# Expert matrices read as neighbouring rows per partition, with a gather of every eighth feature, in a two-layer diffusion trunk

## The reference

```python
N_EXPERTS, N_GROUPS, EXPERTS_PER_GROUP, TOP_K, EXPERT_FF = 16, 4, 4, 2, 512

def moe_ffn(h, router_w, router_b, w1, w3, w2):      # w1, w3: (16, 1024, 512); w2: (16, 512, 1024)
    t = h.reshape(-1, shape[-1])                     # (256, 1024)
    gates = route(t, router_w, router_b)             # (256, 16), two entries not zero per token
    for e in range(N_EXPERTS):
        y = (jax.nn.silu(t @ w1[e]) * (t @ w3[e])) @ w2[e]
        out = out + gates[:, e:e + 1] * y

for i in range(DEPTH):                               # two layers
    x = x + g1 * mixer(...)                          # attention and short convolution, or Conformer convolution
    x = x + g2 * moe_ffn(modulate(rms_norm(x, norm2_g[i]), sh2, sc2), router_w, router_b, w1[i], w3[i], w2[i])
```

## Time and profile before

| | |
|---|---|
| median of 3 runs | 1104.04 us (1101.06 to 1104.61) |
| the profiled execution | 1102.05 us, its span 1100.3 us |
| TensorE matmul busy | 993.9 us, 90% of the span |
| TensorE weight load busy | 789.4 us, 72% |
| VectorE, ScalarE busy | 776.9 us (71%), 624.0 us (57%) |
| DMA | 300.83 MB, 273 GB/s on average |
| mean granted TensorE clock | 0.954 |

### The profile page before, as it was taken

How to read it: one execution, slowest core, us unless ns; L and a number is a source line. 1 busy time by engine, 2 the same in 40 slices (tenths; PEclk the granted TensorE clock), 3 DMA queues, 4 the chain that set the end, 5 groups by cost and what they waited for, 6 DMA issues and landing times.

```text
span 1100.3 us, 17266 instructions
## 1 busy us (share of the span) xinstructions
PE 993.9 (90%) x6128; PEld 789.4 (72%) x6128; DVE 776.9 (71%) x956; ACT 624.0 (57%) x762; POOL 86.9 (8%) x150
## 2 busy tenths in 40 slices
PE   3899989886999999999986998855999999999994
PEld 1588864755888888888864884835888888888873
DVE  1643278447998989989945534644998988978893
ACT  3523326225778778777733423323777778767672
POOL 4090000000000000000000632000000000000000
PEclk8899999997999999999998999876999999999998
DMA  9997864378999999999949965406998998997861
GB/s 336 327 276 227 266 216 137 133 276 280 361 345 310 353 348 317 358 317 351 349 152 361 264 201 178 153 0 212 336 351 318 352 347 312 353 356 236 283 248 40
DMA packets 143035, 300.83 MB, mean 273 GB/s; under 512 B 13461, under 2 KB 44325, under 8 KB 142962
## 3 DMA queue, kind: packets, MB, share of 16 engines
q1 hardware_dynamic: 135360, 286.53, 74.4%
q0 software_dynamic: 6080, 12.66, 4.1%
q10 hardware_dynamic: 1530, 0.78, 0.3%
HBM read 292.35 MB, written 2.92 MB: 268 GB/s over the span
## 4 chain that ended last, share of the span: by engine, by line
PE 81%; DVE 9%; DMA 3%; issue 3%; ACT 2%; SPq 0%; DVEq 0%; ACTq 0%
PE ps L1578 16%; PE ps L1580 16%; PE ps L1579 16%; PE ps L1829 3%; DMA raw<-in_w_mod 3%; PE ps L2051 3%; PE ps L1680 2%; PE ps L1682 2%; PE ps L1681 2%; PE ps L1590 2%; PE ps L1698 1%; PE ps L2073 1%; PE ps L2074 1%; PE ps L2075 1%; PE ps L1700 1%
## 5 line engine op out<-in xcount | busy, mean ns | idle before, releaser
L1318 DVE TENSOR_TENSOR wlo<-raw,whi 128x1024 fp32r<-128x1024 f32 x384 | 456.9, 1221 | 50.7 <-ACT whi L713 48.6
L713 ACT CAST whi<-raw 128x1024 fp32r<-128x1024 f32 x384 | 397.0, 1052 | 105.1 <-PE ps L1580 104.5
L1578 PE MATMUL ps<-whi,xghi 128*128 128x512 f32 x480 | 194.1, 404 | 13.7 <-DVE xglo L1324 13.7
L1580 PE MATMUL ps<-wlo,xghi 128*128 128x512 f32 x480 | 191.8, 400 | 0.0
L1579 PE MATMUL ps<-whi,xglo 128*128 128x512 f32 x480 | 191.8, 400 | 0.0
L1017 DVE TENSOR_TENSOR wlo<-raw,whi 128x1024 fp32r<-128x1024 f32 x56 | 73.8, 1359 | 62.2 <-ACT whi L708 62.2
L1578 PEld LDWEIGHTS ps<-whi,xghi 128*128 128x128 f32 x480 | 91.5, 191 | 35.5 <-issue 13.7
L1580 PEld LDWEIGHTS ps<-wlo,xghi 128*128 128x128 f32 x480 | 91.3, 190 | 22.1
L1579 PEld LDWEIGHTS ps<-whi,xglo 128*128 128x128 f32 x480 | 91.6, 191 | 21.2
L1578 PE MATMUL ps<-whi,hidThi 128*128 128x512 f32 x256 | 102.2, 399 | 1.4 <-issue 1.4
L1580 PE MATMUL ps<-wlo,hidThi 128*128 128x512 f32 x256 | 101.4, 396 | 0.0
(11 more groups left out here) (314 smaller groups left out, 1503.3 us busy)
## 6 DMA issues: line engine op xcount, KB each, us to landing
raw<-in_moe_w SPq DMA_DIRECT2D x384, 512.0 KB, 5.2
raw<-in_w_mod SPq DMA_DIRECT2D x96, 512.0 KB, 6.4
raw<-in_na_w_in SPq DMA_DIRECT2D x24, 512.0 KB, 9.0
raw<-in_cf_pw_w SPq DMA_DIRECT2D x24, 512.0 KB, 8.2
mods<-mod_scratch POOLq DMA_DIRECT2D x9, 512.0 KB, 5.0
raw<-in_ab_w_out SPq DMA_DIRECT2D x8, 512.0 KB, 4.8
urep<-uT SPq DMA_DIRECT2D x64, 35.5 KB, 3.3
urep<-uT POOLq DMA_DIRECT2D x64, 35.5 KB, 3.6
```

What stands on the lines that cost most here:

```text
L713: A.copy(whi[:, (MOE_W[tn.L] + j) % SPL, :], raw[:, (MOE_U[tn.L] + j) % RAW, :]).then_inc(tn.sem("w_rounded"), 1)
L1318: V.tensor_tensor(wlo[:, n % SPL, :], raw[:, (MOE_U[L] + j) % RAW, :], whi[:, n % SPL, :], ALU.subtract).then_inc(tn.sem("unit_done"), 1)
L1578: T.matmul(dst, lhi, rhi, start=first, stop=False)
L1580: return T.matmul(dst, lhi, rlo, start=False, stop=last)
```

## The change

The first and third matrices of the experts (w1, w3) are read so that partition p of chunk k holds feature 8p+k: a partition's share of a unit is two neighbouring rows, 4 KB in one run of device memory, and the runs of two partitions begin 16 KB apart. The gather follows: chunk k takes the features k, k+8, k+16 and so on, which puts 8p+k into partition p. The stationary operand of its matmuls is now a view of `htok` with a step of 8 floats.

```diff
                     else:
-                        src = src[0].rearrange("(k p) n -> p k n", p=P)[:, 2 * q:2 * q + 2, :]
+                        src = src[0].rearrange("(p k) n -> p k n", p=P)[:, 2 * q:2 * q + 2, :]
                         dst = raw[:, slot, :].rearrange("p (k n) -> p k n", k=2)
                     eng.dma_start(dst, src).then_inc(tn.loaded_sem(j), 16)
...
+                def every(t, k):
+
+                    return htok[:, t, :].rearrange("p (m k) -> p k m", k=KC)[:, k, :]
+
                 def gather(tile):
...
-                            ins = T.matmul(dst, htok[:, t, k * P:(k + 1) * P], sel, start=(t == 0), stop=(t == NT - 1))
+                            ins = T.matmul(dst, every(t, k), sel, start=(t == 0), stop=(t == NT - 1))
...
-                            ins = T.matmul(dst, htok[:, t, k * P:(k + 1) * P], pick[:, t, (GROUPS - 1 + e) * P:(GROUPS + e) * P],
+                            ins = T.matmul(dst, every(t, k), pick[:, t, (GROUPS - 1 + e) * P:(GROUPS + e) * P],
```

## The result

| | before | changed |
|---|---|---|
| median of 6 runs | 1104.1 us | 1145.88 us (1144.03 to 1150.33) |
| profiled execution, its span | 1102.05, 1100.3 us | 1144.03, 1142.3 us |
| mean granted TensorE clock | 0.954 | 0.956 |

The ratio is 1.0386, 95% interval 1.0362 to 1.0410: some 42 us slower. The forecast was no change (1103); the range ended at 1143. What happened is the first rival. The median lies 6 us above its estimate of 1140, the profiled execution 4 us; both are inside its 1134 to 1146.

A forecast was written before the change was run, and what follows sets the result against it. The prediction took TensorE to bound the kernel, with DMA hidden behind it. Its terms summed 0 + 0 + 0 + 0 on the profiled 1102.05 us, taken as 1103 us (no change, chance 0.52), range 1099 to 1143.

The forecast's parts named there:

- the first rival: The 12 gathers, 32 loads each: slower by the strided weight load, 1140 us (1134 to 1146); chance 0.39.
- The bound: Expert loops: TensorE never waits, busy 223.80 of 223.80 us over three turns; transfers wait for buffers.
- The pieces: Expert loads of w1 and w3: 128 pieces of 4 KB replace 256 of 2 KB; 0 us, since TensorE covers it.
- SP's queue: Issue of the transfers: one more register step in places, 37 ns each; 0 us given 417 us of waiting there.
- the row order inside the contraction: Expert matmuls, casts and remainders: chunk k holds features 8p+k, shapes stay the same; 0 us.
- The gather, choice of the end: Loads of `htok` in the 12 gathers: the low end, +0 us, taken by a small margin over +38.
- The gather, high end: Loads of `htok`: each column costs double, a pair 208 ns, a gather 6.67 us; sum +38 us (+32 to +44).
- The second: Expert loops: faster because fewer packets interfere less with TensorE's matmuls; a gain of 5 us, 1097; chance 0.06.
- third: Expert loads: scattered addresses drop the rate under 337 GB/s and DMA becomes the bound; +93 us, 1195; chance 0.03.
- fourth rivals: Expert loads: pieces could stay 2 KB, time as forecast; held unlikely, part of the 0.52 for no change.
- the strided load: Gathers: reading `htok` at 32 bytes apart slows the stationary operand's load; +38 us, 1140; chance 0.39.

## Why the prediction was wrong

- **The bound.** Right. TensorE never pauses in the loops, before and after, and of the gathers' 43.5 us the two expert stages show 42.4.
- **The pieces: 0 us.** Right: 32,768 packets fewer, turns of 74.60 us with pieces of 4 KB. The expected relief was nearly absent: with the gather as before the share went from 0.94 to 0.93, and the 0.89 of the changed kernel is mostly the longer turn (0.93 x 74.60 / 78.66 = 0.88).
- **SP's queue, the row order inside the contraction: 0 us.** Right as far as the rows show; the queue waited 458.4 us.
- **The gather, choice of the end: wrong, and this is the step that failed.** The prediction put it so: "A path that already runs at half of what the engine shows elsewhere has room for a fetch of its own for each float." The premise was sound, one column per 0.85 ns, but a line costs about 1.8 ns, over twice that. A slow path is evidence of room only when the cost of what it is to do more often is known, and no row had it. What the trace did show was that nothing hides a longer load. The interval from +0 to +44 had no row inside it, and I took its cheap end on an argument by analogy.
- **The gather, high end: right mechanism, two sizes off.** A pair at the full clock was put at 208 ns (twice 104) and took 238: ten gathers brought 40.3 us in place of 31. The first gathers of the layers were put at +7 between 0.7 and 12.8 (12.7 by its own rows) and brought 3.2. At granted clocks of 0.60 and 0.69 a pair takes 248 ns, hardly more than 238. If it went by TensorE's cycles, the 7.62 us of a gather would be 11 to 13 there (an estimate from these rows), so the time of a line does not. The two errors offset each other in part, 43.5 in all against 38.
- **The Trainium skill's rule.** By its page "Advanced Engine Details and Errata", section "Memory Cachelines", a line of 16 bytes with a single hit does not absorb the latency of the memory, which pointed to the high end; that case got a chance of 0.39 for want of a row. The runs agree with it for the gather: the doubling falls between 8 and 16 bytes, two hits are enough (3.77 against 3.57 us), one is not (7.46). They do not agree for a moving operand of 512 rounded floats: with a step of 2 it has two hits in every line and takes twice as long all the same, 458 against 234 ns. The measurement decides.
- **The second, third and fourth rivals.** The windows refuse the second and third: TensorE's pace did not change with the packets, and the scattered pieces were fast enough. The packets refuse the fourth: the pieces did merge.
- **The chances.** Slower had 0.42. With the loads uncovered and a rule that spoke against the change, the strided load should have been the forecast, or the range should have reached the end of its bounds, 1146; it stopped at 1143.

No version here beats the kernel before: its gather already reads columns side by side, and its transfers were hidden.

## What to carry to other kernels

Before you widen the pieces of a transfer, look whether anybody waits for it; here nobody did, and the price went to the engine that everybody waits for. A layout "(p k)" of the weights moves the step to the activations: if it is the stationary operand, keep it to two floats (deal out pairs of chunks, as in the kernel with a step of 2, where the transfers have the same 4 KB pieces), or put it where an engine has time. Count the 16-byte lines that an operand of TensorE opens, not its columns, for the moving operand most of all, since a long product hides a slow load and nothing hides a slow stream: there even a step of two floats doubled the product.

## What the runs showed of the hardware

- A line of 16 bytes costs a read of TensorE about 1.8 ns (1.74 to 1.86), for loads and for moving operands, for float32 and rounded floats, at steps of 2 to 8 floats. A load of neighbouring columns is bound by its columns, 0.85 ns each, and its lines don't show.
- That time does not stretch with TensorE's clock: a gather with a step of 8 takes 7.92 us at granted clocks of 0.60 and 0.69, and 7.62 at 1.00. With neighbouring columns it takes 6.26 to 6.42 us at 0.58 to 0.59, and 3.57 at 1.00.
- Behind a product of 512 columns (234 ns) a load of 128 lines is hidden: the products keep 0.23 to 0.24 us.
- VectorE's two instructions on 1024 floats, given a step of 128 floats in the tile that they write (the second reads it so, too), went from 1281 and 1225 to 1980 and 1928 ns.
- Pieces of 4 KB in place of 2, 32,768 packets fewer for the same bytes, lowered the queue's share of the DMA engines from 74.4% to 73.5% where the gather kept its pace.
